# Transposing the roles of weights and activations in the large products of a two-layer block: tokens as rows, 512 weight columns moving

## The reference, cut to what matters

```python
# first layer
hn = rmsnorm(x, norm1_w)
y_a, y_b = f(hn)                                   # Hyena branch, mLSTM branch, 1024 features each
gate_a, gate_b = sigmoid(hn @ w_ga), sigmoid(hn @ w_gb)          # 2048 -> 2048 each
mixed = gate_a * (y_a @ w_branch_a) + gate_b * (y_b @ w_branch_b)
x = x + mixed @ w_out
hn2 = rmsnorm(x, norm2_w)
gu = hn2 @ w_gate_up                                # 2048 -> 2 x 5632
x = x + (silu(gu[:, :5632]) * gu[:, 5632:]) @ w_down
x = rmsnorm(x, norm_f_w)
# second layer
n = rms_norm(x, attn_norm_g)
x = x + concat(g(n @ w_in_2)) @ w_out_2             # GLA half, NSA half
m = rms_norm(x, ffn_norm_g)
out = x + (silu(m @ w_gate_2) * (m @ w_up_2)) @ w_down_2
```

## Time and profile before

| | |
|---|---|
| median of three runs | 2871.86 us |
| the profiled execution | 2873.04 us |
| its span | 2871.3 us |
| mean granted TensorE clock | 0.986 |
| PE / weight load / DVE / ACT / POOL busy | 97% / 96% / 54% / 43% / 43% |
| matmuls | 22552 |
| HBM read | 483.67 MB, 169 GB/s |

### The profile page before, as it was taken

The page is one execution under the profiler, slowest core; times in us unless marked ns, Lnnn a source line. Parts: engine busy times, 40 slices in busy tenths (PEclk is TensorE's granted clock), DMA queues, the critical chain, the costliest instruction groups (busy, mean ns, idle before and its releaser), DMA issues.

```text
span 2871.3 us, 52255 instructions
## 1 busy us (share of the span) xinstructions
PE 2784.5 (97%) x22552; PEld 2742.9 (96%) x22552; DVE 1563.3 (54%) x1927; ACT 1227.3 (43%) x1567; POOL 1237.0 (43%) x590
## 2 busy tenths in 40 slices
PE   7999999999999999999999978989999999999999
PEld 7999899999999999999999968989999999999999
DVE  7998755654554443244456777646564442344432
ACT  4333344544444443344445445435454443344433
POOL 2555653334454444444445454322354444444443
PEclk9999999999999999999999979999999999999999
DMA  6444444365555555555555433353355555555564
GB/s 226 157 137 165 152 146 168 123 216 177 188 181 190 177 183 189 186 177 187 185 187 177 173 106 115 133 178 119 122 174 189 188 180 190 179 189 177 178 202 149
DMA packets 72580, 489.12 MB, mean 170 GB/s; under 512 B 8427, under 2 KB 12172, under 8 KB 14752
## 3 DMA queue, kind: packets, MB, share of 16 engines
q1 hardware_dynamic: 72352, 485.79, 49.5%
HBM read 483.67 MB, written 2.10 MB: 169 GB/s over the span
## 4 chain that ended last, share of the span: by engine, by line
PE 86%; DVE 8%; issue 3%; ACT 2%; POOL 1%; DMA 0%; DVEq 0%; ACTq 0%; SPq 0%; POOLq 0%
PE PB L539 26%; PE PB L543 26%; PE PB L540 26%; ACT WH L1063 1%; DVE WL L1491 1%; DVE TM L2174 1%; PE PB L564 1%; DVE TM L2171 1%; PE PB L567 1%; PE PB L566 1%; PE PB L756 0%; PE PB L645 0%; DVE TM L1534 0%; PE PB L659 0%; DVE TM L1542 0%
## 5 line engine op out<-in xcount | busy, mean ns | idle before, releaser
L2272 POOL TENSOR_TENSOR WL<-RAW,WH 128x1024 fp32r<-128x1024 f32 x442 | 1082.2, 2449 | 1442.7 <-ACT WH L1063 1442.5
L539 PE MATMUL PB<-HNH,WH 128*128 128x256 f32 x4768 | 1368.3, 287 | 21.1 <-ACT WH L1063 11.1
L543 PE MATMUL PB<-HNH,WL 128*128 128x256 f32 x4768 | 1357.3, 285 | 6.7 <-DVE WL L1491 3.4
L540 PE MATMUL PB<-HNL,WH 128*128 128x256 f32 x4768 | 1356.5, 285 | 0.0
L1063 ACT ACTIVATE WH<-RAW 128x1024 fp32r<-128x1024 f32 x892 | 923.0, 1053 | 827.3 <-PE PB L543 797.4
L1491 DVE TENSOR_TENSOR WL<-RAW,WH 128x1024 fp32r<-128x1024 f32 x450 | 751.5, 1671 | 864.9 <-ACT WH L1063 864.5
L539 PEld LDWEIGHTS PB<-HNH,WH 128*128 128x128 f32 x4768 | 923.1, 194 | 31.7 <-issue 18.8
L543 PEld LDWEIGHTS PB<-HNH,WL 128*128 128x128 f32 x4768 | 922.5, 193 | 8.4 <-DVE WL L1491 4.8
L540 PEld LDWEIGHTS PB<-HNL,WH 128*128 128x128 f32 x4768 | 922.9, 194 | 1.2 <-issue 0.5
L539 PE MATMUL PB<-HDH,WH 128*128 128x256 f32 x1408 | 396.2, 281 | 0.0
L540 PE MATMUL PB<-HDL,WH 128*128 128x256 f32 x1408 | 396.2, 281 | 0.0
(11 more groups left out here) (326 smaller groups left out, 2713.5 us busy)
## 6 DMA issues: line engine op xcount, KB each, us to landing
RAW<-in_w_gu SPq DMA_DIRECT2D x176, 1024.0 KB, 4.9
RAW<-in_w_dn SPq DMA_DIRECT2D x88, 1024.0 KB, 4.9
RAW<-in_w_in_a SPq DMA_DIRECT2D x57, 1024.0 KB, 4.9
RAW<-in_w_in SPq DMA_DIRECT2D x45, 1024.0 KB, 4.9
RAW<-in_w_out SPq DMA_DIRECT2D x32, 1024.0 KB, 4.9
RAW<-in_w_ga SPq DMA_DIRECT2D x24, 1024.0 KB, 4.9
RAW<-in_w_gb SPq DMA_DIRECT2D x24, 1024.0 KB, 4.9
XT<-in_xT SPq DMA_DIRECT2D x8, 512.0 KB, 7.7
```

Of the source, the lines that this page charges most:

```text
L539: e.matmul(o, WH[:, s, c], hi[:, k, :], start=n == 0, stop=False)
L540: e.matmul(o, WH[:, s, c], lo[:, k, :], start=False, stop=False)
L543: t = e.matmul(o, WL[:, s, c], hi[:, k, :], start=False, stop=last)
L2272: e.tensor_tensor(WL[:, u % NSPL, :], RAW[:, n % NRAW, half * SU * 128:(half + 1) * SU * 128], f32(WH[:, u % NSPL, :]), ALU.subtract).then ...
```

## The change

Branch gates, branch products, output projections and both feed-forwards turn their roles: 128 tokens of an activation tile are stationary, and 512 columns of the weights move. The other stages (`w_in`, the mixers, `w_in_2`) stay as they were.

- A group (`group`) makes 512 output features for both halves of the tokens: two main banks, each 128 tokens x 512 features. Over a block of 16 weight tiles (two units) it goes: half 0 over unit 0 and unit 1, half 1 over unit 0 and unit 1, with four `k` steps of three matmuls each half. A unit is released only in half 1. The hooks run at the start of a block.
- The weights are packed for it on the host (`groups`). The number and size of the weight DMAs, and the splitting, stay.
- The outputs have tokens on partitions, so that 1/rms is one number per partition (`RTOK`): the scale goes into ACT's sigmoid or silu and into DVE's product, which read PSUM directly. The residual is kept as `X` [128 tokens, 2, 2048].
- What is to be the next product's input must have features on partitions: PE turns each 128x128 block with a transpose against the identity (`turn`, eight per group of 512 features) into side banks, and ACT and DVE split it from there.
- Squares are taken by ACT with its accumulator (`token_squares`); sums over 4 groups by DVE on [128, 2]-sized data. The matmuls with ones, the sums on POOL and the multiplication by RF on POOL go. The weight of the norm between the layers is loaded as a broadcast row (`GNF`, four DMAs of 256 KB).
- The output is stored in 8 DMAs instead of 16.

```diff
+            def group(nt, hi, lo, K, ready=None, hooks={}):
+                for n in w.tiles(4 * K):
+                    if n % 4:
+                        continue
+                    p, q = divmod(n, 16)
+                    h, pair = divmod(q // 4, 2)
+                    if q == 0 and p in hooks:
+                        hooks[p]()
+                    if n == 8 * h:
+                        main_free(nt + h)
+                    u = (w.i - q) // SU + pair
+                    s, x, o = u % NSPL, slice(h * 128, (h + 1) * 128), mb(nt + h)[:, 0:512]
+                    for r in range(2):
+                        k, c = 4 * p + 2 * pair + r, slice(r * 512, (r + 1) * 512)
...
+                        e.matmul(o, hi[:, k, x], WH[:, s, c], start=k == 0, stop=False)
+                        e.matmul(o, lo[:, k, x], WH[:, s, c], start=False, stop=False)
...
+                        t = e.matmul(o, hi[:, k, x], WL[:, s, c], start=False, stop=k == K - 1)
+                    steps = ([("nt", nt + h)] if k == K - 1 else []) + ([("unit", u)] if h else [])
+            def turn(name, src, g, wait):
+                for q in range(2):
+                    b = wide_bank(*name, g, q)
+                    for h in range(2):
+                        if q == 0:
+                            wait(h)
+                        for i in range(2):
+                            k = (0 if src is SIG else 512 * g) + 128 * (2 * q + i)
+                            t = e.transpose(b[:, 256 * i + 128 * h:256 * i + 128 * h + 128], src[:, h, k:k + 128],
+                                            IDENT[:, :])
```

The feed-forward on the tensor engine, and the vector engine's part of a hidden group:

```diff
+                for j in range(11):
+                    nt = NT[gu] + 4 * j
+                    group(nt, HNH, HNL, 16, None if j else hn_ready(stage),
+                          {1: lambda: turn_hidden(stage, j - 1) if j else turn_x(stage, ("x", before), 3)})
+                    group(nt + 2, HNH, HNL, 16)
...
+                    run(64)
+                    for h in range(2):
+                        nt = NT[gu] + 4 * j + 2 + h
+                        e.wait_ge(*wt.pe.done("nt", nt))
+                        e.wait_ge(*m.act.done("silu", stage, j, h))
+                        e.scalar_tensor_tensor(out=SIG[:, h, :], in0=mb(nt)[:, 0:512], scalar=RTOK[:, h:h + 1],
+                                               in1=SIG[:, h, :], op0=ALU.mult, op1=ALU.mult).then_inc(
+                                                   *m.dve.mark(("z", stage, j, h), ("free", nt)))
```

More of the change, by code:

```diff
@@ L496, in sync @@
             run(16 * 8)
[L497 to L505, removed]
+            run(22 * 64)
+            for g in range(4):
+                run(4 * 44)
+                for h in range(2):
+                    e.wait_ge(*m.dve.done("x", "dn2", g, h))
+                    e.dma_start(out[:, h, columns(g)], X[:, h, columns(g)]).then_inc(stored, 16)
+            e.wait_ge(stored, 128)
         def tensor(e):
@@ L952, in mixed_ready @@
             def mixed_ready(k):
[L953 to L978, removed]
@@ L1389, in scalar @@
[L1389 to L1403, removed]
-                        if j == 0:
-                            e.wait_ge(*wt.pe.done("nt", NT[dn[0] if half else before] + 15))
-                        e.wait_ge(*m.dve.done("s", stage, half, j))
-                        e.activation(SG[:, j % 2, :], TM[:, nt % 4, :], ACT.Silu).then_inc(
-                            *m.act.mark(("silu", stage, half, j)))
-                        e.wait_ge(*m.dve.done("z", stage, half, j))
-                        e.activation(HDH[:, j, :], TM[:, nt % 4, :], ACT.Copy).then_inc(
-                            *m.act.mark(("hd", stage, half, j)))
[L1412 to L1415, removed]
@@ new lines, in mixed, with normed_turned @@
+            def mixed(g):
+                if g == 0:
+                    e.wait_ge(*wt.pe.done("nt", NT["ga"] + 15))
+                    e.wait_ge(*ml.dve.done("end"))
+                for q in range(2):
+                    e.wait_ge(*m.pe.done("mx", g, q))
+                    k = 4 * g + 2 * q
+                    e.activation(flat(MXH[:, k:k + 2, :]), bank("mx", g, q)[:, :], ACT.Copy).then_inc(
+                        *m.act.mark(("mx", g, q)))
+            def normed_turned(stage, gain, g):
+                for q in range(2):
+                    e.wait_ge(*m.pe.done("hn", stage, g, q))
+                    for i in range(2):
+                        normed(stage, 4 * g + 2 * q + i, gain, bank("hn", stage, g, q)[:, 256 * i:256 * i + 256])
@@ new lines, in after @@
+            def after(n, at, *steps):
+                for k in tiles(n):
+                    if k == at:
+                        for step in steps:
+                            step()
+            for g in range(4):
+                run(64)
+                for h in range(2):
+                    if g == 0:
+                        e.wait_ge(*m.dve.done("o", 7))
+                        e.wait_ge(*m.dve.done("rtok", 0))
+                    branch_gate("ga", g, h)
+                run(32)
+            w.rest()
@@ new lines, in vector @@
+            w.rest()
+            for g in range(4):
+                after(64, 22, *([lambda: mixed(g - 1)] if g else []))
+                run(32)
+                for h in range(2):
+                    nt = NT["gb"] + 4 * g + 2 + h
+                    e.wait_ge(*wt.pe.done("nt", nt))
+                    e.wait_ge(*m.act.done("gate", "gb", g, h))
+                    e.tensor_tensor(SIG[:, h, :], SIG[:, h, :], mb(nt)[:, 0:512], ALU.mult).then_inc(
+                        *m.dve.mark(("free", nt)))
+                    e.wait_ge(*m.dve.prev())
+                    e.tensor_tensor(MIX[:, h, columns(g)], SIG[:, h, :], MIX[:, h, columns(g)], ALU.add).then_inc(
+                        *m.dve.mark(("mix", g, h)))
@@ L2559 @@
     w = one["w_out_2"]
-    a["w_out2"] = units(np.concatenate([tiles(w[0:1024]), tiles(w[1024:2048])]))
-    a["w_gu2"] = gated(one["w_gate_2"], one["w_up_2"])
-    a["w_dn2"] = down(one["w_down_2"])
+    a["w_out2"] = np.concatenate([groups(w[0:1024]), groups(w[1024:2048])])
+    a["w_gu2"] = groups(one["w_gate_2"], one["w_up_2"])
+    a["w_dn2"] = groups(one["w_down_2"])
     a["filt_w1"] = np.ascontiguousarray(one["filt_w1"])
@@ L2607 @@
     got = r.results[0]["out_x"]
[L2608 removed]
+    return np.ascontiguousarray(got.transpose(1, 0, 2)).reshape(1, 256, 2048)
```

513 lines of the change are left out of this document (291 added, 222 removed), and 3 rows, old and new, of the table count.

## The result

The kernel with the change takes **2808.11 us** (median of 4 runs, 2807.52 to 2812.20) against 2871.86 us of the kernel before (2869.03 to 2874.02, likewise 4 runs). The ratio is 0.9782 with a 95% interval of 0.9765 to 0.9799: 2.2% faster, where 5.3% was forecast, and above the range of 2700 to 2765. The profiled execution took 2807.5 us, 65.5 less than the one before, where the sum said 151.7 less.

A forecast was written before the change was run, and what follows sets the result against it. PE was taken as the bound, by the distance between matmul starts, with stationary loads hidden under 512 columns. Terms -186.7 + 34.0 - 0.9 - 2.1 + 3.5 + 0.5 = -151.7 gave 2720 us, range 2700 to 2765.

The forecast's parts named there:

- I take 0.216: Large products: 8256 matmuls of 512 columns at 0.216 us each, 1783.3 us in place of 1970.0, saving 186.7 us.
- A fixed cost per matmul: Rival, 7%: 12 to 13 ns stay with each large-product matmul, 0.2266 us each, +87.5, giving 2808 us.
- Turns, +34.0: Turning activations on PE: 304 transposes at 0.112 us, all on the path, adding 34.0 us.
- Four matmuls with ones, -0.9: Smaller things on PE: four matmuls with ones go, 4 x 0.215, saving 0.9 us.
- The turn waits 0: Evacuation: the turn, one block (5.2 us) into the next group, finds DVE's z done at 2.5 us; cost 0.
- 0 for the main bank: Evacuation: next group's half 1 starts at 2.6 us, its bank is freed at 1.8; cost taken as 0.
- The second layer's seam, +3.5: Start of second layer: the turn stands only 4 tiles in, so PE stalls 3.5 us, between 1 and 6.
- `mn`, -2.1: Seam at mn: PE's waits of 1.2 + 0.9 us for splits and norm go, saving 2.1 us.
- Splits hidden: Weight splitting on ACT, DVE and POOL: 4.9 of 6.5 us look-ahead needed, down from 8.6 available, so no cost.
- Stalls at every group: Rival, 12%: POOL doubles DVE's gated-product operations, PE waits 1.2 us at about 50 groups, +60, 2780 us.
- Slower: Rival, 3%: columns keep today's pace, 512 take 0.2398 us, nothing saved and turns added, +196.5, 2917 us.
- Much faster: Rival, 1%: wide matmuls overlap and cost less than their columns; weight DMAs then bound, -709, 2011 us.

The follow-up runs named there:

- e1_two_of_256: The changed kernel with each 512-column matmul issued as two of 256 columns on the same stationary tile: 2912.69 us, ratio to before 1.0142.
- every form run: Kernels computing nothing of the reference, PE alone running matmuls of 17 and 16 forms (type, widths): fp32r of 512 columns 226.7 ns, bf16 215.8.

## Why the prediction was wrong, and where it was right

**The step that failed** is in "What bounds the kernel now": "What fits both is a load of the stationary tile that takes some 0.11 to 0.12 us of its own: hidden under 0.213 us, bare under 0.107." From it came the term "I take 0.216". It measured 0.2267, so 8256 x 0.0107 = **88 us** of the 186.7 were not there. The whole error, 151.7 against 65.5, is 86.2.

Three things went wrong in that step. The half-clock rows do exclude cycles of the array, a longer column and, taken alone, a fixed number of nanoseconds. I had listed the causes that I could think of, struck out two, and took what was left for shown. The measured fact is one that was not on the list: a price per fp32r matmul, with its load, that is there at 2.4 GHz and not at 1.2, and that stays the same when the columns double. Then the two rows in support were of other forms. The 15-column ones show a floor that ends between 192 and 256 columns, and the fp32 ones a type that pays 2.5 ns where fp32r pays 13.3; both fitted by chance, because the floor of 112 lies so near to 107 + 13. And I put the row of another type ahead of the sum's own most direct neighbours, the 256-column rows with their 12 to 13 ns; the whole weight of the forecast stood on which of the two a 512-column matmul resembles. 7% was far too little for the rival that simply carried those 12 to 13 ns over.

**"A fixed cost per matmul"** (2808) was right in mechanism and in price, 0.2266 against 0.2267. That it meets the median to the microsecond is partly luck, since its other terms were off by 12 to 14 us each way:

- Turns, +34.0: 304 transposes at 0.109 are 33.1 in the trace, and doubling them cost 34.5. Right.
- Four matmuls with ones, -0.9: each is two records on PE, and eight records at 0.215 went (12 of line 584 before, 4 of line 642 after), 1.7 us. The sum had half of it.
- "The turn waits 0", and 0 for the main bank: right in the feed-forwards, the output projection and `mn`, where PE shows no wait at all. Wrong in `ga`: 4.9 us for the bank. With the 4.0 us for POOL's splits and 2.9 more by which the stage is longer than its matmuls and waits add up to (1.0 of them the slower starts behind the nine pauses), `ga` is +11.8, never priced. I had worked out DVE's gated product in the feed-forward and assumed that the branches were the same; in them DVE also carries the mixer's side work.
- The second layer's seam, +3.5: measured 1.9. The wait of 3.1 us for the first scaled row, which was to stay, is gone too, and the NSA side work waits 3.1 us less for GG (7.8 for 10.9) and 1.3 less for TM; these four make 9.1. New small waits stand against them, so the lengths are the better measure: the stretch is 5.2 us shorter, where the sum had it 4.0 longer (3.5 for the stall, 0.9 for eight turns, less two of the matmuls with ones). That is 9.2 us better than the sum. All waits in it together fell by 3.0 us (50.1 to 47.1) and PE's busy time by 2.4 at the higher clock, so a part of the 9.2 may be the clock's and not the change's.
- `mn`, -2.1: both waits are gone. Right. So was the tail, +0.5: from the start of DVE's last residual (2802.5) to the end are 3.2 us, for 2.7 before.
- Splits hidden, with slack shrunk from 8.6 to 6.5 us: right in the feed-forwards and the output projection. Wrong in `ga`, where PE waits six times for POOL's, 4.0 us. DVE's split fell from a mean of 1.67 us, having the spread, to 1.30; the DMA share rose only to 0.55 or 0.56, since the products did not become as fast as thought.

With the other two matmuls with ones (0.4) and the 2.9 us of clock in the first stage, 88.1 + 11.8 - 0.9 - 9.2 - 0.4 - 2.9 = 86.5, and the whole error is 86.2: 0.3 us stay unassigned. One sum behind the range was off as well: 0.2133 per matmul and no seam cost make 2694, not 2700. It changes nothing, since 2808 lies above the range.

**"Stalls at every group"** was wrong in what it put first. DVE's operations that read PSUM were not doubled beside POOL; the gated product takes 743 ns, and the others on 128x512 stayed at what the earlier trace rows has:

```profile
L2279 DVE SCALAR_TENSOR_TENSOR TM<-PB,RTOK,TM 128x512 f32<-128x512 f32 x44 | 30.9, 743 | 0.0
L2203 DVE TENSOR_TENSOR HDL<-PB,HDH 128x512 fp32r<-128x512 f32 x44 | 28.3, 686 | 13.7 <-ACT HDH L1496 13.7
L2223 DVE TENSOR_TENSOR X<-PB,X 128x512 f32<-128x512 f32 x32 | 20.6, 682 | 9.2 <-PE PB L582 9.2
```

What it named as the place, the main bank of the next group, was the place in `ga`, in three of its groups. In front of the product stood the mixer's reciprocals once, and twice a split of DVE drawn out to 2.0 and 2.6 us with mixer work behind it; so a longer operation did play a part, but it was the split, which reads SBUF alone, and not the product. **"Slower"** falls with e1_two_of_256: a 512-column matmul is not two of 256, which cost 2912.7 us, near that rival's 2917; the changed kernel's take 0.2267 us each. **"Much faster"** falls with every form run: none is below its columns.

**Left open.** Why an fp32r matmul pays 13.3 ns at full clock only. The runs exclude accumulation, partitions, the moving address and the surroundings, and a load that 512 columns would hide. They do not show what it is. It may belong to the load: every matmul of every run has one, and the stationary width does change the price, downwards at 256 moving columns and upwards at 512. It may belong to the matmul. Nor do they show why PE waits 4.0 us for POOL's splits in `ga`.

## What to carry to other kernels

A time per instruction has to come from the same data type and the same clock: here one fp32 row at the right array time outweighed thousands of fp32r rows at half the width, and more than half of the forecast gain hung on it. Where "columns plus something" is all that is known, take the something as a constant that remains, and let another explanation earn its place by a short run of the new form alone. And when a bank or a buffer serves several stages, price its wait in the stage with the busiest evacuating engine, not in the cleanest one.

## What the runs showed of the hardware

- fp32r at 2.4 GHz: columns / 2.4 + 13.3 ns for 256, 320, 384 and 512 moving columns with 128 stationary ones, 16.1 at 448, with a floor of 111.7 ns at 192 and 128. bf16: + 2.5 ns. At 1.2 GHz fp32r shows no addition (426.7 ns at 512).
- Fewer stationary columns make fp32r matmuls of 512 columns slower (228.9 to 231.7 ns for 112 to 16 of them), while at 256 they make them faster, 113.3 ns from 80 columns down.
- fp32 is two records of 429.2 ns each at 512 columns, 3.8 times an fp32r one. A change between fp32r and bf16 costs about 9 ns; between fp32r and fp32 none was seen (at 256 columns 547 ns for 120.0 + 2 x 215.8 = 551.6).
- 512 columns followed by 256 (the form "pair") took 353.3 ns for both, 16.7 over the columns for each, so mixed widths do not escape the price.
